# Mean of squares halved on VectorE before TensorE sums it, and low parts of most weights made by the Pool

## The reference

```python
def rms_norm(x, g):
    r = lax.rsqrt(jnp.mean(xf * xf, axis=-1, keepdims=True) + EPS)
    return (xf * r).astype(x.dtype) * g
# per layer
h = rms_norm(x, g_pre_mix) * (1 + sc1) + sh1
...                                             # input projection, two kinds of attention -> o
x = x + gt1 * rms_norm(jnp.dot(o, w_out), g_post_mix)
h = rms_norm(x, g_pre_mlp) * (1 + sc2) + sh2
u = jnp.square(jax.nn.relu(jnp.dot(h, w_up)))   # hidden width 4096
x = x + gt2 * rms_norm(jnp.dot(u, w_down), g_post_mlp)
```

## Time and profile before

| | |
|---|---|
| median of 3 runs | 3145.56 us |
| time of the profiled execution | 3134.87 us |
| its span, first to last instruction | 3133.1 us |
| TensorE busy | 2945.0 us (94%) |
| VectorE busy | 1318.4 us (42%) |
| ScalarE busy | 965.0 us (31%) |
| Pool busy | 85.6 us (3%) |
| mean granted TensorE clock | 0.951 |

### The profile page before, as it was taken

How to read it: one execution, slowest core, us unless ns; L and a number is a source line. 1 busy time by engine, 2 the same in 40 slices (tenths; PEclk the granted TensorE clock), 3 DMA queues, 4 the chain that set the end, 5 groups by cost and what they waited for, 6 DMA issues and landing times. The chain is left out here.

```text
span 3133.1 us, 48148 instructions
## 1 busy us (share of the span) xinstructions
PE 2945.0 (94%) x19659; PEld 2744.0 (88%) x19675; DVE 1318.4 (42%) x2391; ACT 965.0 (31%) x1944; POOL 85.6 (3%) x79
## 2 busy tenths in 40 slices
PE   6998868899999999999999988788999999999997
PEld 5998657779999999999989966677789999999997
DVE  3124747722633333333451356477045333333334
ACT  4222536633411122211341144366143221111222
POOL 0000011100000000000000000211000000000000
PEclk8999779989999999999999978799899999999999
DMA  8111220013221111111221013101212111111121
GB/s 283 41 56 58 93 97 2 17 55 115 78 68 54 54 67 54 40 67 54 107 78 54 33 56 135 55 2 47 79 64 74 54 40 54 40 45 48 40 82 56
DMA packets 135345, 203.33 MB, mean 65 GB/s; under 512 B 8352, under 2 KB 90320, under 8 KB 134672
## 3 DMA queue, kind: packets, MB, share of 16 engines
q1 hardware_dynamic: 135200, 201.27, 18.7%
HBM read 170.45 MB, written 31.00 MB: 64 GB/s over the span
## 5 line engine op out<-in xcount | busy, mean ns | idle before, releaser
L1520 PE MATMUL ps<-hh,wh 128*128 128x352 f32 x2304 | 758.8, 329 | 14.9 <-DVE wl L1043 11.0
L1522 PE MATMUL ps<-hh,wl 128*128 128x352 f32 x2304 | 746.6, 324 | 0.0
L1521 PE MATMUL ps<-hl,wh 128*128 128x352 f32 x2304 | 745.1, 323 | 0.0
L1520 PE MATMUL ps<-uh,wh 128*128 128x352 f32 x1536 | 500.2, 326 | 4.1 <-DVE modn L1470 2.6
L1521 PE MATMUL ps<-ul,wh 128*128 128x352 f32 x1536 | 493.0, 321 | 0.0
L1522 PE MATMUL ps<-uh,wl 128*128 128x352 f32 x1536 | 492.9, 321 | 0.0
L1520 PEld LDWEIGHTS ps<-hh,wh 128*128 128x128 f32 x2304 | 437.6, 190 | 21.2 <-DVE wl L1043 11.0
L1521 PEld LDWEIGHTS ps<-hl,wh 128*128 128x128 f32 x2304 | 438.8, 190 | 1.3
L1522 PEld LDWEIGHTS ps<-hh,wl 128*128 128x128 f32 x2304 | 437.6, 190 | 0.0
L566 ACT ACTIVATE wh<-raw 128x2048 fp32r<-128x2048 f32 (+1 forms) x90 | 172.0, 1911 | 581.9 <-PE ps L1899 580.9
L1043 DVE TENSOR_TENSOR wl<-raw,wh 128x2048 fp32r<-128x2048 f32 (+1 forms) x90 | 207.6, 2307 | 324.2 <-ACT wh L566 324.2
(11 more groups left out here) (250 smaller groups left out, 3909.4 us busy)
## 6 DMA issues: line engine op xcount, KB each, us to landing
ada_v<-w_ada SPq DMA_DIRECT2D x32, 1024.0 KB, 7.1
raw<-w_up SPq DMA_DIRECT2D x32, 1024.0 KB, 5.1
raw<-w_down SPq DMA_DIRECT2D x32, 1024.0 KB, 5.0
raw<-w_in SPq DMA_DIRECT2D x16, 1024.0 KB, 5.5
x_kept<-xr SPq DMA_DIRECT2D x6, 1408.0 KB, 9.4
xf<-x_kept SPq DMA_DIRECT2D x2, 4224.0 KB, 12.6
x_kept<-xf SPq DMA_DIRECT2D x6, 1408.0 KB, 5.5
xr<-x_kept SPq DMA_DIRECT2D x2, 4224.0 KB, 13.0
```

Of the source, the lines that this page charges most:

```text
L1520: pe.matmul(out, w_hi, m_hi, start=start and k == 0, stop=False)
L1521: pe.matmul(out, w_hi, m_lo, start=False, stop=False)
L1522: return pe.matmul(out, w_lo, m_hi, start=False, stop=stop and k == nk - 1)
```

## The change

VectorE gets `halve_squares`: it adds feature tiles 4 to 7 of `sq` onto 0 to 3, and then 2 to 3 onto 0 to 1, in place. `mean` then multiplies 2 tiles, not 8, in all norms but the three pre-mix ones of layer 0. Each halving has a place of its own in VectorE's order.

`split_lo` of all weight blocks but blocks 0 and 1 of layer 0's input projection and the first two blocks of each output projection moves from VectorE to the Pool, which makes them in the order of the blocks.

```diff
 @block.gpsimd
+            def split_lo(l, n, n0=None):
+                w = w_size(n)
+                pool.wait_ge(sm("w_hi"), (l * NW + n + 1) if n0 is None else n0 + 1)
+                pool.tensor_tensor(wl[slot(l, n)][:, 0:w], raw[slot(l, n)][:, 0:w], wh[slot(l, n)][:, 0:w].bitcast(F32), ALU.subtract).then_inc(sm("w_lo"), 1)
             for l in range(DEPTH):
+                for n in range(2, W_WO0):
+                    split_lo(l, n)
...
                 o_lo(3, 1)
+                split_lo(l, W_WO0 + 2)
+                split_lo(l, W_WO0 + 3)
+                split_lo(l, W_MLP0)
+                def mlp_step(m, last):
+                    n0 = snap(pool, l * NW + W_MLP0 + m * 4)
+                    for b in range(1, 4 if last else 5):
+                        split_lo(l, W_MLP0 + b, n0 + b)
...
+                if l + 1 < DEPTH:
+                    split_lo(l + 1, 0)
+                    split_lo(l + 1, 1)
 @block.vector
+            def halve_squares(l, nu, c):
+                cs = slice(c * CH, (c + 1) * CH)
+                i = npos(l, nu, c) - NCH
+                dve.wait_ge(sm("sq_ok"), npos(l, nu, c) + 1)
+                dve.tensor_tensor(sq[:, 0:4, cs], sq[:, 0:4, cs], sq[:, 4:8, cs], ALU.add).then_inc(sm("sum_ok"), 1)
+                dve.wait_ge(sm("sum_ok"), 2 * i + 1)
+                dve.tensor_tensor(sq[:, 0:2, cs], sq[:, 0:2, cs], sq[:, 2:4, cs], ALU.add).then_inc(sm("sum_ok"), 1)
...
-                    split_lo(l, 1)
+                    halve_squares(l - 1, NPOST2, 2)
                     pre_scale(l, NPRE1, 1)
                     post_norm(l - 1, NPOST2, 2)
                     pre_lo(l, NPRE1, 1)
+                    halve_squares(l, NPRE1, 2)
...
-                split_lo(l, W_WO0 + 2)
-                split_lo(l, W_WO0 + 3)
+                halve_squares(l, NPOST1, 0)
                 post_norm(l, NPOST1, 0)
+                halve_squares(l, NPRE2, 0)
                 pre_scale(l, NPRE2, 0)
+                halve_squares(l, NPOST1, 1)
                 pre_lo(l, NPRE2, 0)
                 post_norm(l, NPOST1, 1)
-                split_lo(l, W_MLP0)
+                halve_squares(l, NPRE2, 1)
+                halve_squares(l, NPOST1, 2)
...
-                    split_lo(l, W_MLP0 + 1, n0 + 1)
                     if first:
                         pre_scale(l, NPRE2, 1)
                         post_norm(l, NPOST1, 2)
                     for q in range(12):
-                        if q == (10 if first else 6):
-                            split_lo(l, W_MLP0 + 2, n0 + 2)
...
+                        if first and q == 1:
+                            halve_squares(l, NPRE2, 2)
...
+                        if last and q == 8:
+                            halve_squares(l, NPOST2, 0)
+                        if last and q == 14 and l + 1 < DEPTH:
+                            halve_squares(l + 1, NPRE1, 0)
+                        if last and q == 16:
+                            halve_squares(l, NPOST2, 1)
-                        if last and q == 21 and l + 1 < DEPTH:
-                            split_lo(l + 1, 0)
+                        if last and q == 22 and l + 1 < DEPTH:
+                            halve_squares(l + 1, NPRE1, 1)
...
+            halve_squares(DEPTH - 1, NPOST2, 2)
 @block.tensor
-                pe.wait_ge(sm("sq_ok"), idx + 1)
+                nk = KT if l == 0 and nu == NPRE1 else 2
+                if nk == KT:
+                    pe.wait_ge(sm("sq_ok"), idx + 1)
+                else:
+                    pe.wait_ge(sm("sum_ok"), 2 * (idx - NCH + 1))
```

More of the change, by code:

```diff
@@ L560, in _ @@
                 o_lo(3, 1)
+                split_lo(l, W_WO0 + 2)
[5 more added lines that the diff above has]
+                        split_lo(l, W_MLP0 + b, n0 + b)
+                mlp_step(0, False)
+                with pool.Fori(1, MSTEPS - 1) as m:
+                    mlp_step(m, False)
+                mlp_step(MSTEPS - 1, True)
+                if l + 1 < DEPTH:
+                    split_lo(l + 1, 0)
+                    split_lo(l + 1, 1)
         @block.scalar
@@ L1178, in _ @@
                         dve.tensor_tensor(fg[:, i, :], ps[:, b, 256:264], bfg[:, :], ALU.add).then_inc(sm("fg_a"), 1)
-                    if ends(q) and n_of(it) + 2 < W_WO0:
-                        split_lo(l, n_of(it) + 2)
                     if u == U_GATE and i == TT:
@@ L1425, in _ @@
                                       hh[:, 4 * h:4 * h + 4, SEQ:TOK].bitcast(F32), ALU.subtract).then_inc(sm("ao_lo"), 1)
-                split_lo(l, W_WO0 + 2)
-                split_lo(l, W_WO0 + 3)
+                halve_squares(l, NPOST1, 0)
                 post_norm(l, NPOST1, 0)
+                halve_squares(l, NPRE2, 0)
                 pre_scale(l, NPRE2, 0)
+                halve_squares(l, NPOST1, 1)
                 pre_lo(l, NPRE2, 0)
                 post_norm(l, NPOST1, 1)
-                split_lo(l, W_MLP0)
+                halve_squares(l, NPRE2, 1)
+                halve_squares(l, NPOST1, 2)
                 def mlp_step(m, first, last):
                     mm = snap(dve, l * MSTEPS + m)
-                    n0 = snap(dve, l * NW + W_MLP0 + m * 4)
                     def u_square(q):
@@ L1472, in mlp_step @@
                     for q in range(24):
[L1473 to L1476, removed]
                         kt, c = (q % 8, q // 8) if last else (q // 3, q % 3)
@@ L1546, in mean @@
                 s = idx % 2
-                pe.wait_ge(sm("sq_ok"), idx + 1)
+                nk = KT if l == 0 and nu == NPRE1 else 2
[3 more added lines that the diff above has]
+                    pe.wait_ge(sm("sum_ok"), 2 * (idx - NCH + 1))
                 pe.wait_ge(sm("ln_ok"), max(0, idx - 1))
-                for k in range(KT):
-                    ins = pe.matmul(ps[:, 4 + s, 0:CH], onesd[:, :], sq[:, k, c * CH:(c + 1) * CH], start=(k == 0), stop=(k == KT - 1))
+                for k in range(nk):
+                    ins = pe.matmul(ps[:, 4 + s, 0:CH], onesd[:, :], sq[:, k, c * CH:(c + 1) * CH], start=(k == 0), stop=(k == nk - 1))
                 ins.then_inc(sm("mean_ok"), 1)
```

## The result

The changed kernel takes 3158.67 us (median of 17 runs, 3146.85 to 3172.45). The kernel before, run beside it, takes 3137.88 us (17 runs, 3132.52 to 3149.74). The ratio is 1.0063, with a 95% interval of 1.0049 to 1.0077: 0.6% or some 20 us slower. The three runs known when the prediction was made had their median at 3145.56, 7.7 us above that of the 17.

The account below looks back on a forecast made before the run. At the means a loop over engines bounds, not TensorE's work despite 94% busy. 2 x 6.4 + 9.5 - 4.8 + 1.8 + 6 = 25.3 us slower: 3160 on the profiled execution, 3171 on the median, 3169 given; range 3155 to 3184.

Parts of the forecast that it names:

- rival 3: VectorE, streaming norm instructions, keeps the port and the Pool's split comes late: 13 us slower, 3158; chance 0.20.
- The mean: TensorE's 21 changed means: 16 passes of 4.47 us become 4 of 1.12, 70 us less work.
- The halving: VectorE's two additions per mean: 1.63 us at 1408 columns, 0.89 at 704, with hand-overs 2.6.
- The split on the Pool: One low-part subtract of 2048 columns on the Pool takes 5.0 us, between ends of 2.1 and 5.1.
- tight place: Four places per layer where the Pool's split of 5.0 us just fits; from 5.5 on they lose time.
- The hold: A Pool split holds VectorE's norm work, with two SBUF inputs, for a whole instruction, 5.0 us.
- MLP start: Output projection to second MLP block: TensorE free at 828.9 instead of 822.5, cost 6.4 us per layer.
- Change of layer: Layer 0 to layer 1, Pool splits of blocks 0 and 1 holding norm work: cost 9.5 us, once.
- End: The last means, with no split near: TensorE done at 3105.2 instead of 3110.0, gain 4.8 us.
- Input projection: Pool splits hold rotary work, TensorE waits 2.0 and 1.7 us: 0.9 lost per layer, 1.8 in all.
- Clock: Clock drop after idle of 7 to 9 us in three stages, 2 us each: 6 us, ends 0 and 10.
- Waits before means: TensorE's idle before means grows to some 96 us against 9, which eats the 70 us saved.

Follow-up runs that it names:

- e9: The changed kernel once more, unchanged, for a second profile: 3158.01 us, ratio 1.0079 to the kernel before.
- e1: The changed kernel with only the halving, all splits back on VectorE at their old places: 3141.21 us, ratio 1.0012 to the kernel before.
- e6: The changed kernel with only the first halving, so TensorE multiplies 4 tiles: 3157.84 us, ratio 1.0065 to the kernel before.
- e4: The changed kernel with the six splits that meet norm work back on VectorE, the other 78 on the Pool: 3138.58 us, ratio 1.0005.
- e3: The changed kernel with the Pool writing zeros instead of subtracting in the six blocks that meet norm work: 3128.18 us, ratio 0.9966.
- e5: The changed kernel with each Pool split issued as 8 subtracts of 256 columns: 3148.08 us, ratio 1.0038 to the kernel before.
- e7: Halving alone, all splits on VectorE, with post-mix 1's halving moved ahead of pre-MLP 0's scaling: 3140.56 us, ratio 1.0009 to the kernel before.
- e2: The changed kernel with only the Pool's splits, means of 8 tiles and no halving: 3154.1 us, ratio 1.0057 to the kernel before.
- e8: The kernel before, with halving only in the last post-MLP norm and each input projection's ninth block split on the Pool: 3134.95 us, ratio 0.9987.

## Why the prediction was right

It said slower, 3160 on the profiled execution, by 25 us against it; the medians lie 20.8 apart (23.4 beside e9), the stages 18.4 (21.9 in e9). The given 3169 came from a first median that lay 7.7 us above the later one, so it is 10 high, three quarters of it from there. The time by itself doesn't pick the mechanism: rival 3 had 3158, closer than my own figure. The traces pick it.

- **The mean**: 16 passes to 4, 70 us less work. With full clock a mean of 4 passes held TensorE for 1.0 us (753.11 to 754.12), where 1.12 was forecast; behind long waits for some 2. So busy time of the means fell by 56.8 us and not by 70. It was worth nothing, as e1 and e6 show.
- **The halving**: 1.623 and 0.892 us measured, 1.63 and 0.89 forecast.
- **The split on the Pool**: 4.57 us alone, 4.76 to 5.10 beside VectorE, 5.0 forecast. No tight place lost time (e4).
- **The hold**: forecast as one whole Pool instruction, with single norm instructions of some 5 us. One of `post_add` took 4.93, and all eight together got 4.35 us longer beside a split of 4.76. The Trainium skill, "SBUF — State Buffer", section Who interferes with whom, has a VectorE instruction with two SBUF inputs contend with a Pool instruction that reads SBUF, not with one that only writes it; the two timelines and e3 agree. The Trainium skill's "GPSIMD Engine Reference", section 3, gives 4497 ns for a float32 add of 2048 columns, which the prediction took for the split, a subtract; measured were 4574 in the input projection and 4628 on average.
- **Rival 3** (VectorE keeps the port while it streams): wrong. The Pool got in between two instructions of the stream, 2.3 us after its first (785.54 and 787.82), 0.1 us after its input was ready (787.74); its split took 4.76 us, when most take 4.6. And e5 shows the turns.
- **MLP start**: forecast +6.4, measured +6.7 and +6.6. TensorE was free at 770.4, 780.5, 804.1 and 828.2 for 770.2, 779.5, 803.6 and 828.9. That is within 1 us, but the stage began 0.9 us earlier than before; counted from its start the places lie 1.1, 1.9 and 1.4 us behind the forecast and the last 0.2, so part of the agreement at the last one is two errors against each other. The wait before pre-MLP 2 was 5.5 us, not 8.6: TensorE got there later, as its four groups ran 1.2 us slower at the dropped clock and the means before them too.
- **Change of layer**: forecast +9.5, measured +9.2 and +9.7. From the first to the last mean's end the timeline gave 79.6 us, measured 79.3 (1547.74 to 1627.08). The halving alone costs 6.3 here in e1 and e4 and 3.5 in e7, the Pool's splits alone 6.7 (e2), so the two don't simply add. That VectorE is held by both splits is in its rows (4.05 for eight where no split is near):

```profile
1583.47 8.00 DVE L1124 SCALAR_TENSOR_TENSOR xr<-y,coef,xr 128x352 f32<-128x352 f32 x8
...
1602.45 8.02 DVE L1089 SCALAR_TENSOR_TENSOR y<-xr,coef,rb 128x352 f32<-128x352 f32 x8 [0.22 <-ACT rb L630]
```

- **End**: forecast -4.8, measured -4.1 and, in the second profile of the same kernel, -0.6. It hangs on whether the clock drops after the first wait (e8 has -0.7 with a drop, e1 -4.1 with none). The forecast has no term for that drop, so the close agreement of the first profile is partly luck.
- **Input projection**: a mis-sized term, forecast +1.8, measured -0.1. The holds were there, VectorE's rows after:

```profile
212.13 0.21 DVE L1203 TENSOR_TENSOR rt<-ps,sintab 128x64 f32<-128x64 f32 x1
212.26 0.22 DVE L1204 TENSOR_TENSOR rt<-ps,sintab 128x64 f32<-128x64 f32 x1
212.51 3.62 DVE L1209 TENSOR_TENSOR ro<-rt,rt 128x64 f32<-128x64 f32 x1
...
244.22 3.09 DVE L1209 TENSOR_TENSOR ro<-rt,rt 128x128 f32<-128x128 f32 x1
```

  The Pool's splits ran from 211.47 to 216.04 and from 242.58 to 247.16. The instructions with one input in PSUM ran on beside the first, the one with two in SBUF stood until it was over. But the split took 4.57, not 5.0, and its result was late by less: TensorE waited 1.58 and 1.18 us, where I had 2.0 and 1.7, against 2.82 before, in each layer.
- **Clock**: the other mis-sized term, forecast 6 us on top of the stages. The granted clock did fall, in the window of layer 0's MLP start (after, then before):

```profile
750.00:830.00 80.00, 60.88 (x304) 53.98 (x303) 64.01 (x86) 37.33 (x51) 9.86 (x2) 0.85 0.22 81
```

```profile
750.00:825.00 75.00, 75.00 (x391) 64.58 (x390) 47.04 (x79) 38.32 (x51) 0.00 (x0) 1.00 0.24 86
```

  but slow matmuls between waits use up time that would have been waited anyway. In the MLP starts and the change of layer what is surely lost is what follows the last mean, and there it was 0.7 to 0.8 us (from the last mean on, 72 matmuls took 12.38 us for 11.71 in the change of layer), some 2 in all. That a drop within a stage costs nothing is not shown: the end came 3.5 us later in e9 with one, the change of layer 2.8 later in e1 than in e7.
- **Waits before means**: forecast some 96 us, measured 75.1. Clock-slowed work took the place of waiting; before pre-MLP 2 that is the 3 us of the point above, for the rest it is argued and not measured.

With 2 for the clock and -0.1 for the input projection the sum is 19.4, against 18.4 and 21.9 in the stages and 20.8 in the medians.

## What to carry to other kernels

Work taken from the busiest engine is time only where its next input is already there: follow one norm through all its engines and add up the loop before counting the gain. Work moved to the Pool isn't free of VectorE, even at 3% load. Where the Pool's instruction reads SBUF and VectorE's has both inputs there, each may wait for a whole one of the other (4.93 us for an instruction of 0.58). So move what falls beside PSUM reads or where VectorE has time to spare, as in the MLP loop here; small pieces make the single hold short (1.05 us in e5), but hold again and again. When six of 84 moved pieces carry the cost, keep those six where they were.

## What the runs showed of the hardware that I had not expected

The granted clock of a stage that is the same code in all kernels varied from run to run. Windows of e1, both layers' sliding-window attention, at 0.81; layer 1 of the kernel before was at 0.73 and 12.6 us longer:

```profile
303.74:447.53 143.79, 116.14 (x1008) 88.94 (x1006) 91.74 (x165) 71.51 (x227) 0.00 (x0) 0.81 0.35 120
1846.21:1989.91 143.70, 116.22 (x1008) 89.08 (x1006) 91.72 (x165) 71.32 (x226) 0.00 (x0) 0.81 0.35 120
```

Over the 12 profiles it took 143.7 to 156.9 us, whatever the kernel. That is more than most effects here, and the likeliest reason why single runs of one kernel lie up to 30 us apart (3129.88 to 3159.59 in e1); it was not shown that it explains the medians of e3. A wait of 2 us before a mean was followed by a drop of the clock in e8 and e9 and by none in e1 and in the changed kernel's first profile, at the same place. What decides that stays open.
